# A decoder step with 32 experts: w_down in runs of 8 KB, and bias products in row strips 64 and 96

## What is computed

```
logits = x2d @ w_router + b_router
top_vals, top_idx = top_k(logits, 4);  gates = softmax(top_vals)
for each block of tokens of expert e:
    xb = x2d[toks]                                  # fetch the block's rows
    gu = xb @ w_gate_up[e] + b_gate_up[e]           # 1024 -> 2048
    g, u = gu[:, :1024], gu[:, 1024:]
    g = min(g, 7);  u = clip(u, -7, 7)
    hid = (u + 1) * (g * sigmoid(1.702 * g))
    out = hid @ w_down[e] + b_down[e]               # 1024 -> 1024
    y[toks] += gate * out
```

## Time and profile before

| | value |
|---|---|
| median of three runs | 1394.33 us (1388.69 to 1396.81) |
| span of the profiled execution | 1390.1 us |
| PE busy in it | 1331.7 us, 96% |
| DVE, ACT, POOL busy | 448.6, 262.0, 86.1 us |
| moved by DMA | 498.42 MB, mean 359 GB/s |
| expert loop, from the first item's gate products to the last item's transposes L1480 | 398.8 to 1358.9 us |

### The profile page before, as it was taken

The page is one execution under the profiler, slowest core; times in us unless marked ns, Lnnn a source line. Parts: engine busy times, 40 slices in busy tenths (PEclk is TensorE's granted clock), DMA queues, the critical chain, the costliest instruction groups (busy, mean ns, idle before and its releaser), DMA issues.

```text
span 1390.1 us, 20690 instructions
## 1 busy us (share of the span) xinstructions
PE 1331.7 (96%) x7774; PEld 511.9 (37%) x7775; DVE 448.6 (32%) x947; ACT 262.0 (19%) x613; POOL 86.1 (6%) x91
## 2 busy tenths in 40 slices
PE   8899998989999999999999999999999999999995
PEld 6355444554533333333333223333333333333221
DVE  1244454655662222222222232222322223222224
ACT  1332334754141101011010011000111001101002
POOL 2022233310002000000000000000000000000000
PEclk9999998997999999999999999999999999999998
DMA  9569589787078999999999998799999999999993
GB/s 361 220 233 354 199 329 363 279 315 258 28 307 332 392 418 416 417 418 418 418 418 418 417 418 359 288 418 419 418 418 418 417 416 417 419 419 418 418 416 116
DMA packets 97093, 498.42 MB, mean 359 GB/s; under 512 B 9869, under 2 KB 11021, under 8 KB 62234
## 3 DMA queue, kind: packets, MB, share of 16 engines
q1 hardware_dynamic: 85398, 430.44, 76.5%
q0 software_dynamic: 11520, 67.11, 12.5%
q10 hardware_dynamic: 132, 0.27, 0.1%
HBM read 493.60 MB, written 3.93 MB: 358 GB/s over the span
## 4 chain that ended last, share of the span: by engine, by line
PE 52%; DMA 9%; SPq 7%; ACT 1%; issue 1%; DVE 0%; ACTq 0%; DVEq 0%
PE psum L2094 24%; PE psum L2141 14%; DMA arena<-in_w_gate_up 9%; SPq L271 7%; PE psum L1473 6%; PE psum L2076 4%; PE psum L1487 2%; PE psum L2125 1%; PE psum L1480 1%; ACT arena L2199 1%; DVE arena L2343 0%; PE psum L2043 0%; SPq L2008 0%; PE psum L2062 0%; DVE arena L2318 0%
## 5 line engine op out<-in xcount | busy, mean ns | idle before, releaser
L2094 PE MATMUL psum<-arena 128*64 128x512 f32 x2112 | 470.9, 595 | 10.2 <-DMA arena<-in_w_gate_up 9.6
L2094 PEld LDWEIGHTS psum<-arena 128*64 128x64 f32 x2112 | 146.5, 137 | 323.5 <-issue 289.9
L2240 DVE SCALAR_TENSOR_TENSOR arena<-psum,arena 128x256 f32<-128x256 f32 (+1 forms) x128 | 110.0, 880 | 456.5 <-PE psum L2076 363.0
L2141 PE MATMUL psum<-arena 128*64 128x512 f32 x1056 | 235.4, 598 | 3.0
L2141 PEld LDWEIGHTS psum<-arena 128*64 128x64 f32 x1056 | 73.5, 138 | 151.0 <-issue 133.4
L2177 ACT ACTIVATE arena<-psum 128x512 f32<-128x512 f32 x33 | 19.7, 597 | 490.6 <-PE psum L1480 490.6
L2287 DVE TENSOR_SCALAR arena<-psum 128x512 f32<-128x512 f32 x33 | 22.8, 692 | 249.9 <-PE psum L2094 249.9
L1473 PE MATMUL psum<-arena 128*64 128x512 f32 (+1 forms) x420 | 103.1, 608 | 0.0
L1196 DVE STREAM_TRANSPOSE arena<-arena 128x1024 f32<-128x1024 f32 x64 | 74.9, 1215 | 1.8 <-DVE arena L1300 0.9
L2076 PE MATMUL psum<-arena 64*128 64x512 f32 x264 | 74.5, 641 | 0.9 <-ACT arena L2203 0.9
L583 PE MATMUL psum<-arena 128*128 128x512 f32 x128 | 63.8, 631 | 3.6 <-DVE arena L1185 3.6
(11 more groups left out here) (268 smaller groups left out, 1027.0 us busy)
## 6 DMA issues: line engine op xcount, KB each, us to landing
arena<-in_w_gate_up SPq DMA_DIRECT2D x256, 1024.0 KB, 18.4
arena<-in_w_down SPq DMA_DIRECT2D x128, 1024.0 KB, 16.8
arena<-in_w_in SPq DMA_DIRECT2D x12, 1024.0 KB, 24.2
arena<-in_w_out SPq DMA_DIRECT2D x4, 1024.0 KB, 9.8
arena<-in_x_prompt SPq DMA_DIRECT2D x4, 512.0 KB, 4.8
out<-arena SPq DMA_DIRECT2D x8, 256.0 KB, 2.1
arena<-in_b_gate_up ACTq DMA_DIRECT2D x66, 4.0 KB
arena<-in_ln_g SPq DMA_DIRECT2D x2, 512.0 KB, 6.8
```

The lines of the kernel that those rows point to most:

```text
L2094: ins = nc.tensor.matmul(psum[64 * h:64 * h + 64, n, :], x_k, slot[k][:, col:col + 512], start=False, stop=(k == KD - 1))
L2141: ins = nc.tensor.matmul(psum[64 * h:64 * h + 64, 4, :], h_k, slot[s][:, col:col + 512], start=(k == 0), stop=(k == KD - 1))
L2240: ins = nc.vector.scalar_tensor_tensor(out=rows, in0=products, scalar=item_gate[:, b, col], in1=rows, op0=ALU.mult, op1=ALU.add)
```

## The change

It has three parts. `w_down` is read so that partition p of a slot has the adjacent rows 2p and 2p + 1 of the 256, one run of 8 KB. To match, each transpose of `hid` takes every second column of a 256-column part, where it took 128 adjacent ones. The bias row and its ones lie on partitions 64 and 96, where they lay on 0 and 32, and in `body` the products of token block 2 are issued behind the four bias products, where they stood ahead of them.

```diff
+BIAS_AT = (64, 96)
...
-                src = a["w_down"][0, bass.ds(e, 1), 2 * j * P:(2 * j + 2) * P, :].rearrange("e (r p) n -> p (e r) n", p=P)
-                dst = (slot[s] if spare is None else spare).rearrange("p (r n) -> p r n", r=2)
+                src = a["w_down"][0, bass.ds(e, 1), 2 * j * P:(2 * j + 2) * P, :].rearrange("e (p r) n -> (e p) (r n)", r=2)
+                dst = slot[s] if spare is None else spare
...
             for h in range(2):
                 for n in range(2):
-                    ins = nc.tensor.matmul(psum[64 * h:64 * h + 64, n, :], ones_rows[32 * n:32 * n + 1, :],
-                                           bias_row[32 * n:32 * n + 1, h * 512:h * 512 + 512],
+                    ins = nc.tensor.matmul(psum[64 * h:64 * h + 64, n, :], ones_rows[BIAS_AT[n]:BIAS_AT[n] + 1, :],
+                                           bias_row[BIAS_AT[n]:BIAS_AT[n] + 1, h * 512:h * 512 + 512],
                                            start=True, stop=False)
...
-                def fetch(t):
+                def fetch_prompt(t):
 
                     pe.wait_ge(pick_ready, 3 * t + 3)
-                    for b in range(3):
-                        ins = fetch_block(b, first=(b == 0), last=(b == 2))
-                    ins.then_inc(fetched, 1)
+                    for b in range(2):
+                        fetch_block(b, first=(b == 0), last=False)
+
+                def fetch_samples():
+
+                    fetch_block(2, first=False, last=True).then_inc(fetched, 1)
...
                     pe.wait_ge(xg_copied, t + 2)
-                    fetch(t + 2)
+                    fetch_prompt(t + 2)
                     pe.wait_ge(gate_clamped, t + 1)
                     pe.wait_ge(e_dve, 2 * t + 1)
                     pe.wait_ge(bias_loaded, 32 * t + 64)
                     add_bias()
+                    fetch_samples()
                     pe.wait_ge(xg_ready, t + 3)
                     pe.wait_ge(hid_ready, t + 1)
+                    pairs = hid.rearrange("p (j q r) -> p j r q", j=2, r=2)
                     for c in range(4):
-                        ins = nc.tensor.transpose(psum[:, 3, c * P:(c + 1) * P], hid[:, c * P:(c + 1) * P], ident)
+                        ins = nc.tensor.transpose(psum[:, 3, c * P:(c + 1) * P], pairs[:, c // 2, c % 2, :], ident)
```

More of the change, by code:

```diff
@@ L1518, in _ @@
                 for n in range(2):
-                    sp.dma_start(bias_row[32 * n:32 * n + 1, :], a["b_gate_up"][0, 0:1, n * D:n * D + D]).then_inc(bias_loaded, 16)
+                    sp.dma_start(bias_row[BIAS_AT[n]:BIAS_AT[n] + 1, :], a["b_gate_up"][0, 0:1, n * D:n * D + D]).then_inc(bias_loaded, 16)
                 for s in range(8, RING):
@@ L2102, in body @@
                         if k == 2 and first:
-                            fetch(1)
+                            fetch_prompt(1)
+                            fetch_samples()
                         if k == 5 and first:
@@ L2171, in load_bias @@
                     for n in range(2):
-                        act.dma_start(bias_row[32 * n:32 * n + 1, :], a["b_gate_up"][0, bass.ds(e, 1), n * D:n * D + D]
+                        act.dma_start(bias_row[BIAS_AT[n]:BIAS_AT[n] + 1, :], a["b_gate_up"][0, bass.ds(e, 1), n * D:n * D + D]
                                       ).then_inc(bias_loaded, 16)
```

## The result

The changed kernel takes 1442.03 us (median of four runs, 1438.69 to 1442.81), the kernel before 1395.57 us beside it (1388.69 to 1396.96, with a fourth run to the three of the table above). The ratio is 1.0335, 95% interval 1.0311 to 1.0359: slower, where slower was forecast, but by 46.5 us and not by 13.2. The profiled execution has a span of 1441.0 us, against 1390.1.

What follows compares the result with a forecast made beforehand. TensorE was taken to bound the loop, with 13.9 us due to DMA. 33 items longer by 0.82 us give 27.1, less 13.9, so +13.2 on 1394.3: 1407.5 us, range 1386 to 1412.

Steps and rivals of the forecast that it cites:

- What bounds the kernel: The loop: TensorE takes 28.85 us an item, DMA 30.44 us an expert; waits for DMA are 13.9 us of 1390.1.
- the sum: Loop: items longer by 0.82 us, 33 times, 27.1 us, less 13.9 us of DMA waits: +13.2 us, 1407.5 us.
- Part 1, a slot of w_down: DMA of w_down in 8 KB runs: 0.08 us less a slot, 0.3 us less an expert, bounds 0 and 0.44.
- The stepped transposes: Transposes of hid ahead of the down products: reading every second column costs 0.05 us an item, 0 to 0.11.
- The drain at a change of height: Between bias and block 2 products: changing strip height empties TensorE on any partitions, block 2's loads a microsecond behind, chance 0.67.
- the overlap on the same rows: In the earlier trace, operand loads go ahead while same-shape products run on the same rows: two 0.14 us loads every 0.43 us.
- The bare copy, 0.77 us an item: Before the transposes of hid: ScalarE's copy loses the cover of the bias products, so the transposes go 0.77 us later.
- The range: Total time from 1386 to 1412 us, reaching from the fastest rival to the upper end of the forecast's own range.
- the rivals: Bias step: block 2 runs beside the bias products, 1386 us, 0.19; partly beside, or under half the price, 1390 to 1395, 0.14.

Runs made afterwards that it cites:

- the runs alone: The kernel before with only w_down in 8 KB runs and hid transposed by every second column; 1373.1 us, ratio 0.9947.
- the order alone: The changed kernel with w_down and the transposes of hid as before, so only bias strips and product order changed; 1428.47 us, ratio 1.0348.
- the wait filled: The changed kernel with an unneeded product between block 2's products and the transposes; 256 columns: 1403.75 us, ratio 1.0161; 320 columns: 1396.91 us, ratio 1.0118.
- the old order: The kernel before with 8 KB runs and ScalarE's copy to xg delayed by an unneeded 904-column operation, so the transposes wait; 1439.58 us, ratio 1.0337.

## Why the prediction was right in direction and wrong in size

- **What bounds the kernel.** Right. Items of 28.85 us on TensorE and 13.9 us of waits for DMA: the waits vanished after the change, as in the sum (13.8 us over the 31 items), and the runs alone gained 7.7 us where 8.4 was worked out for a TensorE that stays at 28.85 us an item.
- **Part 1, a slot of w_down.** Right: 0.3 us an expert expected, 0.31 measured with the runs alone (30.44 to 30.13).
- **The stepped transposes.** 0.05 us an item taken, bounds 0 and 0.11; 0.08 measured (28.93 less 28.85 with the runs alone).
- **The drain at a change of height.** Right, and shown from both sides: 1.02 us between the loads of bias and block 2 in the changed kernel, 0.01 us between their products where they have one height, and no difference between strips 0 and 32 and strips 64 and 96. The rule of the Trainium skill, TensorEngine Tiling (Array Packing), Key Properties, that a change of tiling mode drains TensorE, holds in this case. By the Trainium skill, TensorE: Matmul & The Clock Gate, The mechanism, a load goes ahead of running products where its row group doesn't conflict, or where it goes to the background weight buffer. The first doesn't hold here where the height differs (1.02 us); the second leaves room for the overlap on the same rows, which the prediction held against that page.
- **The bare copy, 0.77 us an item.** Right: 0.76 with the order alone, 3.75 us from the last fetch loads to the transposes as worked out.
- **The sum.** This is the step that failed, by a term that isn't in it: what the clock does once TensorE stands bare. It took the other 29 us of an item to be as long as before, with the clock at 1.00 as in the earlier trace rows. With the item at 29.69, 24 of 31 have 3.4 us at half clock, at 1.38 us each: 33.1 us of a loss of 50.9 in the span, more than the bare copy. The changed kernel with the wait filled is that sum measured without this term: ratio 1.0118, where the forecast was 1407.5/1394.3 = 1.0095.
- **The range.** It ended at 1412 because its upper side held only the errors of the terms listed. A case "the wait costs clock as well" was none of the rivals, though the prediction itself put a gap of 0.7 us among small products that had followed each other without one.

The Trainium skill does have a place for it, TensorE: Matmul & The Clock Gate, A second HAM failure mode: a kernel that idles briefly between groups of matmuls, often enough for the clock to go up and down. The runs agree in kind: 0.53 us an item was enough in the old order. By the Trainium skill, same page, HAM oscillation, on waits for DMA, one would look for much longer gaps than these. The DMA waits of before, 0.54 to 0.57 us before slots 6 and 7, left the clock at 1.00, so the length of a wait doesn't tell: those stand amid products of 512 columns, and the wait for the copy amid transposes and one-row products.

What stays open: what it is in the step that the chip goes by. The runs show that a wait there suffices (27 of 31), that work in its place takes the fall away (24, 5, 0) and that a step without a wait but with little work also has it (8, and 0 with more work). They don't show why one item in four escapes in the changed kernel, though its falls drift through the step and that item follows the earliest of them, nor which of the small products counts how much. That the transposes and one-row products are what makes this step sensitive is argued from the rows, and no run moved the wait elsewhere.

## What to carry to other kernels

When a change makes TensorE wait, even for half a microsecond, ask what it does around the wait: amid small products the clock fell here for 3.4 us, and that cost twice the wait (1.38 us for 0.70), so put it into the sum or at least into the range. Products on different rows ran beside each other here only where their strips had one height; and ahead of a wait, the product that releases the other engine goes first and the one nobody waits for covers it. Of this change the 8 KB runs are worth keeping by themselves: they are ahead of both kernels, at a ratio of 0.9947 to the kernel before, which is 0.5%.

## What the runs showed of the hardware that was not expected

- A wait of 0.53 to 0.70 us an item, in a loop where TensorE is busy for 931.23 of 953.56 us, takes the clock to 1.2 GHz for 3.4 us in 23 to 27 of 31 items. The page's strip shows 9 in all these slices, since the mean is 0.95; the granted clock of short stretches and the distance of loads (0.62 us for 0.29) show it.
- A product that computes nothing of use made the kernel faster: 320 columns an item in the wait, from a ratio of 1.0335 to 1.0118.
- Two products of one height on rows 0 to 63 and 64 to 127 start 0.01 us apart; where one of the two has a single row, their loads stand 1.02 us apart, on strips 0 and 32 as on 64 and 96.
- Transposes that read every second column cost 0.08 us more for four, and a 1 MB slot in runs of 8 KB in place of 4 KB comes 0.08 us sooner (0.31 us for four).
